# Which expert weight units stay unsplit, and when the finished rows leave PSUM

## The reference, cut to what matters

```python
def moe_swiglu(h, w_router, w1, w3, w2):
    logits = (h @ w_router).astype(jnp.float32)
    top_logit, top_idx = lax.top_k(logits, TOP_K)
    gates = jax.nn.softmax(top_logit, axis=-1)
    ...                                   # tokens gathered by expert, in blocks
    def expert_block(args):
        xblk, e = args
        return (jax.nn.silu(xblk @ w1[e]) * (xblk @ w3[e])) @ w2[e]
    yb = lax.map(expert_block, (xb, block_e)).reshape(n_rows, d)
    return jnp.zeros_like(h).at[tok].add(yb * gate[:, None])
```

## Time and profile before

| | us |
|---|---|
| median of three runs | 2679.74 |
| the other two runs | 2675.83, 5290.58 |
| profiled execution | 2679.73 |
| its span | 2677.9 |
| PE busy in the span | 2597.1 (97%) |
| DVE busy | 1819.1 (68%) |
| ACT busy | 1439.4 (54%) |
| mean of the 16 DMA engines' busy share in the expert part | 0.9 and more from about 1670 us on |

### The profile page before, as it was taken

One profiled execution on the slowest core, in us unless ns is written; L12 is line 12 of the kernel. 1 busy time (PEld: TensorE's weight loads), 2 busy tenths in 40 slices (PEclk: granted clock), 3 DMA queues, 4 the chain that ended last, 5 costly groups with the idle time before them and its releaser, 6 DMA issues.

```text
span 2677.9 us, 47122 instructions
## 1 busy us (share of the span) xinstructions
PE 2597.1 (97%) x18358; PEld 2049.7 (77%) x18358; DVE 1819.1 (68%) x2625; ACT 1439.4 (54%) x2065; POOL 0.2 (0%) x4
## 2 busy tenths in 40 slices
PE   8999999999999999999999999999999999999997
PEld 6787777888788888867877898678887666666665
DVE  4876574445422333358765667998989899898897
ACT  5534375223422222355344645777777777787775
POOL 0000000000000000000000000000000000000000
PEclk8999999999999999999999999999999999999998
DMA  7010273224222223210114445999999999999996
GB/s 290 2 50 33 96 268 126 95 96 175 75 104 95 94 95 126 96 62 2 50 48 143 157 183 196 369 406 347 364 352 403 410 414 420 418 422 417 420 421 283
DMA packets 80149, 577.21 MB, mean 216 GB/s; under 512 B 8800, under 2 KB 10208, under 8 KB 10208
## 3 DMA queue, kind: packets, MB, share of 16 engines
q1 hardware_dynamic: 79680, 572.89, 54.5%
q10 hardware_dynamic: 288, 1.74, 0.2%
HBM read 573.54 MB, written 1.05 MB: 215 GB/s over the span
## 4 chain that ended last, share of the span: by engine, by line
PE 75%; DVE 12%; issue 5%; ACT 4%; DMA 3%; DVEq 0%; ACTq 0%; SPq 0%
PE bank L594 71%; DMA ring<-wstream 3%; DVE weights_low L2795 3%; DVE more_weights_low L2795 2%; PE bank L855 2%; ACT weights_high L1638 1%; ACT arena L1638 1%; PE bank L1276 1%; ACT more_weights_high L1638 1%; DVE arena L3084 1%; DVE weights_low L2398 1%; PE bank L1532 1%; DVE arena L2710 1%; PE bank L706 0%; DVE arena L3033 0%
## 5 line engine op out<-in xcount | busy, mean ns | idle before, releaser
L1638 ACT ACTIVATE arena<-bank 128x512 f32<-128x512 f32 (+3 forms) x578 | 275.3, 492 | 709.1 <-PE bank L594 632.6
L1638 ACT ACTIVATE weights_high<-ring 128x1024 fp32r<-128x1024 f32 (+1 forms) x345 | 467.6, 1363 | 252.9 <-PE bank L594 239.1
L2398 DVE TENSOR_TENSOR weights_low<-ring,weights_high 128x1024 fp32r<-128x1024 f32 x220 | 266.7, 1223 | 398.8 <-ACT weights_high L1638 398.7
L594 PE MATMUL bank<-h_low,weights_high 128*128 128x512 f32 (+1 forms) x960 | 347.4, 362 | 0.0
L2795 DVE TENSOR_TENSOR weights_low<-ring,weights_high 128x2048 fp32r<-128x2048 f32 x125 | 285.1, 2285 | 36.6 <-ACT weights_high L1638 36.0
L594 PE MATMUL bank<-arena 64*64 64x64 f32 (+5 forms) x4944 | 267.0, 242 | 15.9 <-DVE arena L2613 4.5
L594 PEld LDWEIGHTS bank<-arena 64*64 64x64 f32 (+3 forms) x4944 | 224.5, 143 | 39.4 <-issue 14.2
L2795 DVE TENSOR_TENSOR more_weights_low<-arena,weights_high 128x2048 fp32r<-128x2048 f32 x87 | 198.8, 2285 | 20.4 <-ACT weights_high L1638 19.1
L594 PEld LDWEIGHTS bank<-h_low,weights_high 128*128 128x128 f32 x960 | 182.0, 190 | 27.4
L594 PE MATMUL bank<-weights_high,tokens_high 128*128 128x512 f32 x544 | 180.6, 420 | 1.0 <-DVEq L2951 1.0
L1638 ACT ACTIVATE weights_high<-arena 128x2048 fp32r<-128x2048 f32 x87 | 165.9, 1907 | 27.1 <-DMA arena<-wstream 13.7
(11 more groups left out here) (342 smaller groups left out, 5110.4 us busy)
## 6 DMA issues: line engine op xcount, KB each, us to landing
ring<-wstream SPq DMA_DIRECT2D x369, 1024.0 KB, 6.1
arena<-wstream SPq DMA_DIRECT2D x171, 1024.0 KB, 8.4
xT<-xin SPq DMA_DIRECT2D x2, 1024.0 KB, 6.3
cn<-consts SPq DMA_DIRECT2D x1, 1576.0 KB, 22.2
sm<-small SPq DMA_DIRECT2D x1, 1568.0 KB, 24.6
sm<-small ACTq DMA_DIRECT2D x1, 1568.0 KB, 11.6
out<-hT SPq DMA_DIRECT2D x2, 512.0 KB, 3.0
cn<-consts ACTq DMA_DIRECT2D x1, 130.0 KB, 2.9
```

The lines of the kernel that those rows point to most:

```text
L594: return nc.tensor.matmul(o, lhsT, rhs, start=first, stop=last)
L1638: return nc.scalar.activation(o, i, func, **kw)
L2398: step(vx.tensor_tensor(ring_low[:, u % RING, cols], ring[:, u % RING, cols], wh[:, j % 4, :].bitcast(F32), ALU.subtract), "weights low", j)
```

## The change

Three things change. The unsplit units are 1, 5, 9, 13, 17, 21, 25, 31 and 37 in place of 2, 7, 11, 15, 19, 23, 27, 33 and 38; there are nine in both lists, seven of them below unit 28. The first three split units of a small pass are so 0, 2 and 3 and no longer 0, 1 and 3. At the end of every pass, small or wide, ScalarE writes the output rows behind `next_high(0)` and ahead of `next_high(1)`, and VectorE writes its two remainders behind the first low part and ahead of the second. The call in front of pass 0 names unit `SPLIT[q]`, which is now unit 2 for turn 1.

```diff
-UNSPLIT = [2] + list(range(7, 2 * PAIRS, 4)) + [33, 38]
+UNSPLIT = list(range(1, 2 * PAIRS - 2, 4)) + [31, 37]
 ...
                 for q in range(AHEAD):
-                    if q == AHEAD - 1:
+                    if q == 1:
                         act.wait_ge(*here("gates kept"))
                         act.wait_ge(*here("spent", MOE_UNITS - 1))
                         for n in range(2):
 ...
             for q in range(1, AHEAD - 1):
                 dve.wait_ge(*done("first high", q))
-                rest(q)
+                rest(SPLIT[q], q)
 ...
                 for q in range(AHEAD - 1):
                     dve.wait_ge(*here("next high", q))
                     rest(split_units(wide_next)[q], q).then_inc(*tick(e_vectors, kind, "next low", q))
-                for n in range(2):
-                    dve.wait_ge(*here("y high", n))
-                    half_of = slice(n * 512, (n + 1) * 512)
-                    vx.scalar_tensor_tensor(yl[:, half_of], bank[6 + n][:], slot_gate,
-                                            ys[:, half_of].bitcast(F32), ALU.mult, ALU.subtract)\
-                        .then_inc(*tick(e_vectors, kind, "y kept", n))
+                    if q == 0:
+                        for n in range(2):
+                            dve.wait_ge(*here("y high", n))
+                            half_of = slice(n * 512, (n + 1) * 512)
+                            vx.scalar_tensor_tensor(yl[:, half_of], bank[6 + n][:], slot_gate,
+                                                    ys[:, half_of].bitcast(F32), ALU.mult, ALU.subtract)\
+                                .then_inc(*tick(e_vectors, kind, "y kept", n))
```

## The result

The changed kernel took 2707.93 us (median of four runs, 2705.53 to 2708.23), against 2678.98 for the one before in the same session. The ratio is 1.0108, 95% interval 1.0095 to 1.012. It is slower by 29 us, outside the range of the prediction (2671 to 2685) and beyond its slower rival (2690.1). The profiled execution took 2708.23 us, its span 2706.4, and that is what is read here against the 2677.9 of before.

What follows compares the result with a forecast made beforehand. It took the weight stream to bound late small passes, TensorE and its feeding engines the wide ones. From 2679.73 us, -3.0 + 1.1 + 0.6 + 0.6 - 0.3 = -1.0 gave 2678.7 us, range 2671 to 2685.

Steps and rivals of the forecast that it cites:

- slower rival: Rival B: VectorE's chain starts 2.1 us later at small boundaries too, 2690.1 us in all; chance 0.13.
- What bounds the small passes: Late small passes: the weight stream at 422 GB/s, 104.4 us for 42 units, with a hole behind the gather.
- Number of units: Whole kernel: nine unsplit units before and now, so the engines and SP's queue have the same work, 0.
- Five small boundaries: In front of passes 4 to 8: +0.9 at unit 6, -1.5 behind unit 12, 0.6 us gained a pass, -3.0.
- 31 and 37: Unsplit 31 and 37 for 33 and 38 give back two slots 1.6 us later: 0, at most +0.6 a pass.
- Boundaries of 0 and 1, 1 and 2: Next to wide passes, the rows delay unit 1's copy and low part: +0.6 and +1.1 us.
- Boundary of 2 and 3: Into the first small pass: full slots, VectorE's chain starts 2.1 us later, less 1.5 by the gather, +0.6.
- Pass 0: Unit 4's copy and low part 1.5 us late, VectorE 0.7 early: -0.3 at the gather, between -3 and +2.
- End: Behind the last pass: VectorE's extra low part is hidden by ScalarE's copy and load of tables, 0.
- A: Rival: holes in the stream behind the gather stay, only the costs remain, 2681.7 us; chance 0.22.
- B: Rival: stream gets ahead at boundaries, ScalarE no longer waits for unit 3, VectorE starts 2.1 us later, 2690.1 us; chance 0.13.
- C: Rival: more relief for VectorE, all holes closed (-4.5) and -3 in pass 0, 2674.5 us; chance 0.25.

Runs made afterwards that it cites:

- run 5: Changed kernel with the transposes of pair 12's hidden values moved behind the gather in small passes; 2685.0 us, ratio 1.0026 to the kernel before.
- run 6: Changed kernel with three extra, unread matmuls filling TensorE's wait ahead of pair 12's transposes; 2696.6 us, ratio 1.0065 to the kernel before.
- run 7: Kernel before the change, with unsplit unit 25 for 27 and pair 12's transposes behind the gather; 2675.1 us, ratio 0.9985.
- run 12: run 5 with unsplit units 33 and 38 put back for 31 and 37; 2682.4 us, ratio 1.0016 to the kernel before.
- run 1: Kernel before the change with the new list of unsplit units alone, output rows left where they were; 2712.1 us, ratio 1.0118.
- run 3: Changed kernel with unsplit unit 27 in place of 25; 2696.6 us, ratio 1.0072 to the kernel before.
- run 4: Kernel before the change with unsplit unit 25 in place of 27, nothing else; 2695.5 us, ratio 1.0059.
- run 10: run 7 with the output rows moved as the change does, unit 1 still split; 2686.5 us, ratio 1.0035 to the kernel before.

## Why the prediction was wrong

**What bounds the small passes: right.** No pass of any run went under 104.2 us, and the hole behind the gather is what could be won or lost.

**Number of units, 0: right.** VectorE and ScalarE were busy for 1820.5 and 1439.7 us, from 1819.1 and 1439.4.

**Five small boundaries, -3.0: wrong, and it is the step that failed.** It had two halves. The first, unit 6 later by 0.9, measured from the gather to the end of the low part of unit 12, was +1.8 in pass 6 of after and +2.2 in run 5 (65.5 us before, 67.3 and 67.7 then): mis-sized. "Nothing lost" up to unit 3 was wrong as well: counted from the gather, its copy started at 37.1 us before and 37.7 after. The second, from that low part to the gather, was put at 38.0 for 39.5, -1.5. Before showed 39.8, run 5 shows 38.2, after 40.1. So the count of the loops was right, and "units 26 and 27, whose parts were made under the plain unit" was the fault. Their parts were ready; the hidden values of pair 12 were not, and TensorE's own order has their transposes ahead of the gather. The prediction followed the units and left out the instruction between the last unit and the gather. In place of -0.6 a pass, after has +2.1 with the wait alone and +5.0 to 5.6 with the fall. Even without the wait, in run 5, a pass is 0.4 longer than before and not 0.6 shorter, by the first half.

**The clock: not in any case.** The text took 1.00 for granted in the expert part, since the rows of before that it read had it. That was not so to the end: behind an idle of 4.4 us that ends at 2656 us, before is at 0.50 from 2660 us on. An added wait was priced at its length. Here 1.4 us of wait cost about 1.8 us a pass by itself (run 6 less run 5) and another 3 us in every second pass. The slower rival had neither this wait nor the clock, and was 18 us short.

**31 and 37, 0 to +0.6 a pass: mis-sized**, about +0.8 a pass on run 7; in the new order 0.4, inside the bounds but not clear of scatter.

**Boundaries of 0 and 1, 1 and 2: right.** +0.7 (forecast +0.6) and +1.2 (forecast +1.1). At the latter TensorE waits for the copy of unit 1 as worked out, and 0.21 us for its low part where 0.5 was forecast; timeline of after:

```profile
1902.68 1.92 ACT L1638 ACTIVATE weights_high<-ring 128x2048 fp32r<-128x2048 f32 x1
1904.65 0.50 PE L594 MATMUL bank<-weights_high,tokens_high 128*128 128x512 f32 x1 [0.50 <-ACT weights_high L1638]
```

**Boundary of 2 and 3, +0.6: the part up to the gates was +0.3; behind it stands pass 3's wait for pair 12. Pass 0, -0.3: right in number, in part by luck** (82.33 us before and 82.06 after, up to its gather). It holds a wait of 1.23 us for a pair's hidden values and one of 2.15 for a low part with a clock of 0.79 behind it, which the count did not have. **End, 0:** the part behind the last gather is 59.2 us before and 64.2 after, but 60.6 in run 6, so 3.6 of it is the lower clock behind the gather of pass 8; the wait for the rows and the one for the squares only changed their shares (4.4 and 2.0 us, then 2.0 and 4.2).

**The rivals.** A said the holes stay: they grew, for another reason. B had the sign, not the mechanism: at the small boundaries of after ScalarE still waits for the transfers of units 2 and 3 (0.67 and 0.50 us in pass 6, 1.82 for unit 3 before). The rows did not run "at once" either, they waited 1.13 us until TensorE was through the last unit:

```profile
2350.50 1.26 ACT L1638 ACTIVATE y_rows_high<-bank,rs 128x512 fp32r<-128x512 f32 x2 [1.13 <-PE bank L594]
2352.43 1.91 ACT L1638 ACTIVATE weights_high<-ring 128x2048 fp32r<-128x2048 f32 x1 [0.67 <-DMA ring<-wstream]
2354.85 1.92 ACT L1638 ACTIVATE more_weights_high<-ring 128x2048 fp32r<-128x2048 f32 x1 [0.50 <-DMA ring<-wstream]
```

C's relief, 4.5 us of closed holes, is about what run 7 got (3.9 us), by another edit.

**The sum as measured.** Clock 11.3 + wait for pair 12 with its hole 11.6 + units 31 and 37 2.6 + the rest 4.1 (run 12 less before) = 29.6, against 29 measured. These are differences along one chain of kernels, so that they add up is no test of them. Of the rest, the trace of run 12 has 1.7 us at the boundaries of 1 and 2 and of 2 and 3, and 0.9 behind the last gather.

What stays open: why the clock fell behind the wait in three passes and not in the other three. The waits have the same length, within 0.03 us. It is open in the same way for another idle: a wait of 2.15 us for a low part in pass 0 has a clock of 0.66 to 0.83, in the lowest 5 us, beside it in after and in runs 1, 3, 6 and 12, and 1.00 in run 5.

## What to carry to other kernels

When the order of work changes, follow every instruction between the moved unit and the next milestone on the waiting engine, above all the small ones that consume a result of the moved unit; a count of the large ones can be right to 0.1 us and the forecast still wrong in sign. A new wait of TensorE can be dearer than its length (here 1.4 us cost 1.8, and 5 with the fall), so price it with the lower clock as well. And where a dependent step can stand behind independent work, move it there before tuning what feeds it: here that edit of two lines was worth 22.9 us in one version and made another the fastest.

## What the runs showed of the hardware that was not expected

An idle of 1.4 us ahead of a gather of small matmuls was followed by TensorE's lower level in 3 of 6 passes of after and 2 of 6 of runs 1 and 4, and never at the gathers of run 6, in which otherwise useless matmuls filled it. With the fall the gather takes 5.0 to 6.1 us for 3.7, and the clock is back at 1.00 within 15 us, with nothing done for it. Waits of 1.26 and 1.11 us one behind the other (run 10) were followed by 0.66 as well, but other such pairs of the run by 1.00. And a stream of 1 MB transfers kept 421 and 422 GB/s over whole passes of 104.3 and 104.5 us (run 7).
